# A sliding-window attention cut into 32 overlapped units, with half of its output product beside them

## What is computed

```python
def sliding_window_gqa_sinks(q, k, v, sinks):
    ...
    scores = jnp.einsum("bnqkgd,bnskd->bnkgqs", qb, kb) * scale
    scores = jnp.where(mask, scores, -jnp.inf)
    m = jnp.maximum(jnp.max(scores, axis=-1, keepdims=True), sink)
    p = jnp.exp(scores - m)
    denom = jnp.sum(p, axis=-1, keepdims=True) + jnp.exp(sink - m)
    out = jnp.einsum("bnkgqs,bnskd->bnqkgd", p / denom, vb)
...
h = h + (attn * jax.nn.silu(z)) @ w_out + b_out
h = rms_norm(h, final_norm_g)
hn = rmsnorm(h, norm_w[i])
proj = hn @ w_in[i]
```

## Time and profile before

| | us |
|---|---|
| median of 3 runs (3640.29 to 3643.76) | 3641.27 |
| the profiled execution | 3642.55 |
| its span, first to last instruction | 3640.7 |
| PE busy, of the span | 3226.1 |
| DVE busy | 1650.6 |
| ACT busy | 1090.1 |
| POOL busy | 830.5 |

### The profile page before, as it was taken

How to read it: one execution, slowest core, us unless ns; L and a number is a source line. 1 busy time by engine, 2 the same in 40 slices (tenths; PEclk the granted TensorE clock), 3 DMA queues, 4 the chain that set the end, 5 groups by cost and what they waited for, 6 DMA issues and landing times.

```text
span 3640.7 us, 37492 instructions
## 1 busy us (share of the span) xinstructions
PE 3226.1 (89%) x15228; PEld 2508.5 (69%) x15228; DVE 1650.6 (45%) x2650; ACT 1090.1 (30%) x1814; POOL 830.5 (23%) x655
## 2 busy tenths in 40 slices
PE   8999899999998999999996659789876898889978
PEld 6766676668777777788874437677754777667746
DVE  6977621124455443413344553476753344331233
ACT  2135531123411211233224431444431222221134
POOL 3210011114155642253110001111100223221211
PEclk9999899999999999999997789899988999789989
DMA  3110011114122321233110001210103233321111
GB/s 118 41 35 18 7 35 47 41 63 158 59 74 81 92 80 47 85 115 131 41 35 18 6 30 64 83 29 24 47 28 88 65 101 84 130 92 37 37 52 58
DMA packets 240171, 225.40 MB, mean 62 GB/s; under 512 B 14720, under 2 KB 197376, under 8 KB 238976
## 3 DMA queue, kind: packets, MB, share of 16 engines
q1 hardware_dynamic: 220720, 180.84, 16.4%
q10 hardware_dynamic: 19280, 42.18, 3.2%
HBM read 184.25 MB, written 38.73 MB: 61 GB/s over the span
## 4 chain that ended last, share of the span: by engine, by line
PE 67%; DVE 12%; ACT 7%; POOL 6%; issue 5%; DMA 2%; ACTq 0%; SPq 0%; DVEq 0%; POOLq 0%
PE psum L499 17%; PE psum L501 16%; PE psum L500 16%; PE psum L505 4%; PE psum L614 3%; POOL arena L2876 3%; POOL WS L2802 2%; DVE arena L2185 1%; DVE arena L2451 1%; DVE arena L2471 1%; PE psum L660 1%; PE psum L871 1%; PE psum L686 1%; ACT arena L1559 1%; PE psum L1066 1%
## 5 line engine op out<-in xcount | busy, mean ns | idle before, releaser
L2802 POOL TENSOR_TENSOR WS<-arena,WS 128x1024 fp32r<-128x1024 f32 x239 | 590.8, 2476 | 2305.5 <-ACT WS L1083 2305.4
L499 PE MATMUL psum<-XH,WS 128*128 128x512 f32 x2464 | 991.3, 402 | 36.8 <-POOL XL L2858 15.9
L500 PE MATMUL psum<-XL,WS 128*128 128x512 f32 x2464 | 967.7, 393 | 0.0
L501 PE MATMUL psum<-XH,WS 128*128 128x512 f32 x2464 | 967.7, 393 | 0.0
L499 PEld LDWEIGHTS psum<-XH,WS 128*128 128x128 f32 x2464 | 469.1, 190 | 154.6 <-issue 42.1
L501 PEld LDWEIGHTS psum<-XH,WS 128*128 128x128 f32 x2464 | 467.6, 190 | 100.2
L500 PEld LDWEIGHTS psum<-XL,WS 128*128 128x128 f32 x2464 | 469.1, 190 | 97.6 <-issue 4.3
L1083 ACT ACTIVATE WS<-arena 128x1024 fp32r<-128x1024 f32 x239 | 251.0, 1056 | 846.5 <-PE psum L501 333.0
L499 PE MATMUL psum<-WS,XH 128*128 128x512 f32 (+1 forms) x1024 | 402.5, 393 | 49.8 <-POOL WS L2802 35.5
L500 PE MATMUL psum<-WS,XH 128*128 128x512 f32 (+1 forms) x1024 | 397.1, 388 | 0.0
L501 PE MATMUL psum<-WS,XL 128*128 128x512 f32 (+1 forms) x1024 | 397.1, 388 | 0.0
(11 more groups left out here) (293 smaller groups left out, 3256.8 us busy)
## 6 DMA issues: line engine op xcount, KB each, us to landing
arena<-in_w_in SPq DMA_DIRECT2D x85, 512.0 KB, 3.8
arena<-in_w_in_even SPq DMA_DIRECT2D x48, 512.0 KB, 4.1
arena<-in_w_out SPq DMA_DIRECT2D x32, 512.0 KB, 3.3
arena<-in_w_out_even SPq DMA_DIRECT2D x32, 512.0 KB, 3.3
h_spill<-arena ACTq DMA_DIRECT2D x24, 512.0 KB, 3.4
arena<-h_spill ACTq DMA_DIRECT2D x12, 1024.0 KB, 9.2
arena<-s_table SPq DMA_DIRECT2D x8, 1536.0 KB, 6.8
arena<-in_w_in_odd SPq DMA_DIRECT2D x18, 512.0 KB, 3.8
```

Of the source, the lines that this page charges most:

```text
L499: e.matmul(ps, wh, xh, start=start, stop=False)
L500: e.matmul(ps, wh, xl, start=False, stop=False)
L501: return e.matmul(ps, wl, xh, start=False, stop=stop)
L2802: e.tensor_tensor(lo, raw(book.raw_of.get(("w", u), 0), kbs, n), hi.bitcast(F32), SUB).then_inc(*w.up("w_lo", u))
```

## The change

**The units.** The 16 steps of eight heads become 32 units of four heads, numbered by block of tokens first: four units (g, and which half of its heads) for block 0, four for block 1, and so on. They overlap by position in a common loop `attention2` of 37 rounds, called ticks here. In tick u, PE makes the scores of unit u, the transposes of u - 2 and the values of u - 3; DVE does the maximum of u, the division of u - 1 and the gating of u - 4; ACT copies the transposed probabilities of u - 2 (now both blocks of keys) and takes the exponentials of u. The buffers for probabilities are three, those for transposed ones two. PSUM banks are given as before: 0 to 3 to scores (two per unit), 4 and 5 to transposes (two per unit), 6 to the values, 7 to the products beside them.

**The work beside.** The four late z blocks do their first half before the loop and their second half in ticks 1, 3, 5 and 7. The output product of the first four token tiles runs inside the loop, one tile of 24 matmuls in each of the ticks 17, 19, 21, 23 (first 512 outputs) and 27, 30, 33, 34 (second). The engines that follow PE do their part one tick later. The product of the last four tiles follows the loop with `proj_th`.

**Splits, loads and norms.** ACT and POOL split `Z2` by blocks of tokens, in every fourth tick from 8 to 36; h comes back from DRAM by halves (ticks 16 and 32) into the space of the queries. The norms go by halves of the tokens too: `od_post(0)` beside the product of the last four tiles, `od_post(1)` after it and after the transposes of half 0.

```diff
+        UNITS = [(n, g, hq) for n in range(8) for g in range(2) for hq in range(2)]
+        PRU, PTU = [view(84 + 4 * i, 4, 256) for i in range(3)], [view(96 + 4 * i, 2, 512) for i in range(2)]
+        STU = [view(104 + i / 16, 12) for i in range(3)]
+        BO2, G2 = view(72, 2, 512), view(76, 2, 512)
+        SQ2 = [view(80, 2, 512), view(100, 2, 512)]
+        XS3 = view(84, 4, S)
+        FILL = (1, 3, 5, 7, 17, 19, 21, 23, 27, 30, 33, 34)
+        def H2(tile):
+            return QT[:, 2 * (tile % 4):2 * (tile % 4) + 2, half_of(tile // 4)]
+        def blocks_of(u):
+            return ([1], 128) if UNITS[u][0] == 0 else ([0, 1], 0)
+        def attention2(tick, fill, late):
+            for u in range(37):
+                tick(u)
+                if u - late in FILL:
+                    next(fill, None)
+            run(fill)
...
+            late = [load_w(w2[:, 1792 + 128 * i:1920 + 128 * i], 8, 128) for i in range(4)]
+            def z_tile(i, half, ring):
+                u, hl = late[i]
+                bank = take(ring, ("z2o_ps", 4 + i, half), ("z2o", 4 + i, half))
+                w.wait_ge("w_lo", u)
+                sl = half_of(half)
+                for kb in range(8):
+                    t = mm3(psum[:, bank, :], hl[0][:, kb, :], hl[1][:, kb, :], XH[:, kb, sl], XL[:, kb, sl], kb == 0, kb == 7)
+                t.then_inc(*w.up("z2o_ps", 4 + i, half, also=[("w_used", u)] if half else []))
+            for i in range(4):
+                z_tile(i, 0, pb)
...
+            def values2(u):
+                n, g, hq = UNITS[u]
+                kbs = blocks_of(u)[0]
+                bank = take(ob2, ("o2", u), ("zo2", u))
+                for kb in kbs:
+                    w.wait_ge("t2_out", u, kb)
                 w.wait_ge("v2", 7)
-                for p in range(2):
-                    for kb in kbs:
-                        t = e.matmul(psum[64 * p:64 * p + 64, bank, :], V2[:, n - 1 + kb, 64 * g:64 * g + 64],
-                                     pt_of(g, n)[:, 2 * p + kb, :], start=kb == kbs[0], stop=kb == 1)
-                t.then_inc(*w.up("o2", g, n))
-
-            def attend(g):
-                for n in range(8):
-                    if n and g == 0:
-                        output2(g, n - 1)
-                    scores2(g, n)
-                    if n and g == 1:
-                        output2(g, n - 1)
-                    yield
-                output2(g, 7)
-                yield
-            weave((attend(0), 1, True),
-                  (proj_cm("z2o_ps", (), w2, 1792, 4, b7, lambda m, half: [("z2o", m, half)], base=4), 1, True))
-            w.mark("od_a0")
-            run(attend(1))
-            w.mark("od_a1")
-            for event in (("od_a0", "act"), ("od_a0", "dve"), ("zo2", 1, 7)):
-                w.wait_ge(*event)
-            run(proj_tm("o3_ps", (0,), ap["w_out_odd_2"], 0, 512, pb, lambda tile: [("o3a", tile)], x="odo"))
-            run(proj_tm("o3_ps", (1,), ap["w_out_odd_2"], 512, 512, pb, lambda tile: [("o3b", tile)]))
-            w.mark("od")
-
-
-            turn_x("b3", view(52, 4, S))
+                for kb in kbs:
+                    for p in range(2):
+                        t = e.matmul(psum[64 * p:64 * p + 64, bank, 0:256], V2[:, n - 1 + kb, 64 * g:64 * g + 64],
+                                     PTU[u % 2][:, kb, 256 * p:256 * p + 256], start=kb == kbs[0], stop=kb == 1)
+                t.then_inc(*w.up("o2", u))
...
+            def tick(u):
+                if u < 32:
+                    scores2(u)
+                if 2 <= u < 34:
+                    turned2(u - 2)
+                if 3 <= u < 35:
+                    values2(u - 3)
+            def z_late():
+                for i in range(4):
+                    z_tile(i, 1, b7)
+                    ws.free()
+                    yield
+            w3 = ap["w_out_odd_2"]
+            attention2(tick, chain(z_late(), *[
+                proj_tm("o3_ps", (ch,), w3, 512 * ch, 512, b7, lambda tile, ch=ch: [("o3", ch, tile)], tiles=range(4),
+                        ready=lambda tile: ("odo", tile)) for ch in range(2)]), 0)
+            for ch in range(2):
+                run(proj_th("o3_ps", (ch,), w3, 512 * ch, 1, lambda tile: [("o3", ch, tile)], x="odo"))
...
+            def turned2(u):
+                for kb in blocks_of(u)[0]:
+                    w.wait_ge("t2", u, kb)
+                    if u >= 2:
+                        w.wait_ge("o2", u - 2)
+                    e.activation(PTU[u % 2][:, kb, :], ps_of("t2", u, kb), ACT.Copy).then_inc(
+                        *w.up("t2_ca", u, kb, also=[("t2_out", u, kb)]))
...
+            def tick(u):
+                if 2 <= u < 34:
+                    turned2(u - 2)
+                if u < 32:
+                    powers(u)
+                if u >= 8 and u % 4 == 0:
+                    n = u // 4 - 2
+                    w.wait_ge("zo2", u - 5)
+                    w.wait_ge("z2o_ps", 7, n // 4)
+                    e.activation(XH[:, :, tile_of(n)], Z2[:, :, tile_of(n)], ACT.Copy).then_inc(*w.up("x_hi", "odo", n))
+                if u == 16:
+                    load_h2(0, 15)
+                if u == 32:
+                    load_h2(1, 31)
+                    e.dma_start(BO2, row_in("b_out").rearrange("p (a b) -> p a b", a=2)).then_inc(*w.landed("od_rows", 0))
+                    e.dma_start(G2, row_in("final2").rearrange("p (a b) -> p a b", a=2)).then_inc(*w.landed("od_rows"))
+            def fill():
+                for i in range(4):
+                    z_ev(4 + i, 1)
+                    ws.free()
+                    if i == 3:
+                        for _ in range(4):
+                            ws.load()
+                    yield
+                for ch in range(2):
+                    for tile in range(4):
+                        if tile == 3:
+                            for _ in range(4):
+                                ws.free()
+                            if ch == 0:
+                                for _ in range(4):
+                                    ws.load()
+                        yield
+            attention2(tick, fill(), 1)
...
+            weave((chain(proj_th(), proj_th()), 1, True), (od_post(0), 1, True))
+            turn_half("b3", 0, lambda kb: col("norm_w_3", kb), [])
+            run(od_post(1))
+            turn_half("b3", 1, lambda kb: col("norm_w_3", kb), [])
...
+            def gated2(u):
+                n, g, hq = UNITS[u]
+                z = Z2[:, 4 * g + 2 * hq:4 * g + 2 * hq + 2, tile_of(n)]
+                w.wait_ge("o2", u)
+                for k in range(2):
+                    w.wait_ge("z2o", 4 * g + 2 * hq + k, n // 4)
+                e.tensor_tensor(z, z, psum[:, book.bank("o2", u), 0:256].rearrange("p (a b) -> p a b", a=2), M).then_inc(
+                    *w.up("zo2", u))
+            def tick(u):
+                if u < 32:
+                    weigh(u)
+                if 1 <= u < 33:
+                    divide(u - 1)
+                if 4 <= u < 36:
+                    gated2(u - 4)
...
+            def od_post(hf):
+                for j in range(7):
+                    tile = 4 * hf + j
+                    if j < 4:
+                        h = H2(tile)
+                        w.wait_ge("od_rows")
+                        w.wait_ge("o3", 1, tile)
+                        e.tensor_tensor(h, h, BO2, A_).then_inc(*w.up("o3_b", tile))
+                    if 1 <= j < 5:
+                        h, r = H2(tile - 1), small[:, 31 + tile:32 + tile]
+                        nrm_recip("odf", tile - 1, r)
+                        w.own()
+                        e.scalar_tensor_tensor(h, h, r, G2, M, M).then_inc(*w.up("h2", tile - 1))
+                    if j < 4:
+                        nrm_mean("odf", tile, small[:, 32 + tile:33 + tile], 1e-5)
+                    if 2 <= j < 6:
+                        nrm_mean("b3", tile - 2, small[:, 2 * tile - 4:2 * tile - 3], 1e-6)
+                    if j >= 3:
+                        r = small[:, 2 * tile - 6:2 * tile - 5]
+                        nrm_recip("b3", tile - 3, r)
+                        w.own()
+                        if hf:
+                            w.wait_ge("turn", "b3", 7, 0)
+                        e.tensor_scalar(XS3[:, j - 3, :].rearrange("p (a b) -> p a b", a=2), H2(tile - 3), r, None, M).then_inc(
+                            *w.up("nrm_xs", "b3", tile - 3))
+                    yield
+            run(od_post(0))
+            for ch in range(2):
+                for tile in range(4, 8):
+                    o3(ch, tile)
+            turn_half("b3", 0, lambda kb: col("norm_w_3", kb))
+            run(od_post(1))
+            turn_half("b3", 1, lambda kb: col("norm_w_3", kb))
...
+            def tick(u):
+                if u >= 8 and u % 4 == 0:
+                    n = u // 4 - 2
+                    w.wait_ge("x_hi", "odo", n)
```

(2 more changed lines are left out.)

390 lines of the change are left out of this document (168 added, 222 removed).

## The result

The changed kernel takes 3657.44 us (median of 6 runs, 3653.93 to 3660.11), the kernel before 3642.49 (6 runs, 3640.25 to 3648.63). The ratio is 1.0039, with a 95% interval of 1.0026 to 1.0052: slower by 0.26% to 0.52%. I had forecast 3608, with a range of 3585 to 3634.

A forecast was written before the change was run, and what follows sets the result against it. PE bounds most of the kernel, but a chain of dependences sets the second attention's time. Terms 272.1 + 5.5 + 2 + 9 + 50.2 + 31.8 = 370.6 us against 403.6, -33, gave 3608 us, range 3585 to 3634.

The forecast's parts named there:

- step 1: Attention loop: each tick is a full round of scores, DVE's whole tick and values, 6.24 us per unit of four heads.
- The rival that this round isn't there: Attention loop: values not held by the gating, about 4.05 us a tick, about 3545 us in all; chance 0.04.
- step 5: Attention loop: part of the ticks run at the lower clock, 1.9 us more each; +9 us (0 to 59).
- The rival of the half clock: Attention loop: clock stays at half, all 31 ticks cost 1.9 us more, 59 instead of 9, 3658 us; chance 0.05.
- steps 3 and 4: Attention loop: ACT's four weight splits at tick 24 delay the next division, +5.5 us; one VectorE division held behind POOL, +2.
- step 6: Output product's last four tiles, after the loop: PE waits 4.5 us for block 7's split; 50.2 us in all.
- step 7: From the output product's end to the third layer's first product: 31.8 us against 30.0, halving the norms gains nothing.
- That nothing outside the stretch changes: Rest of the kernel: no edit touches anything outside the stretch, so only the stretch's time was forecast to change, by -33 us.
- the stretch: From the second attention's first scores to the third layer's first product: 370.6 us forecast against 403.6 before.

## Why the prediction was wrong, point by point

**The round of waits (step 1)** was right: 6.23 us against 6.24, with PE's values released by the gating in every tick from 4 to 31. That it fits to the hundredth is luck, as the values took 1.08 where I had 0.94 and small errors in the other terms gave it back. The gating took 0.41 (estimated 0.42). The rival that this round isn't there fell. What I didn't do was to ask what it would take to remove it; one line did.

**The clock (step 5)** is the step that failed, in its size. I had +9 us for the whole loop. In ticks 9 to 31, the fifteen ordinary ticks were 6.89 on average, 0.65 over 6.24, in sum 9.7; and the six with a tile were 14.85 against 11.68, in sum 19.0. That is 28.7 in these ticks. The kernel with six extra matmuls takes nearly all of it back: ticks 9 to 30 are 209.0 us in the changed kernel and 183.3 there. What stays is mostly in ticks 10 and 26, which follow the two stalls and are 7.2 and 7.8 us there too, so some 2.5 of the 28.7 are not the clock's. Ticks 0 to 8 are 12 us over the forecast, and 7 of these are three z tiles that start at the half clock (8.4, 7.5 and 7.5 us in ticks 3, 5 and 7, against 5.44).

Two errors are in it. I started from 30% of the ticks, and then halved that because tiles would keep the clock up. They do so for the ticks between them (6.9 us on average, 7.5 in the kernel without tiles), but each tile starts at the half clock and pays more than that for it. And I priced the lower clock only in scores and values, not in the tiles, which are the longest pieces on the path. The share at the half clock stayed at what the earlier trace rows said, 42%.

**The rival of the half clock** had the right mechanism and 0.05 of the chances. I gave it a threshold (22 of 31 ticks) computed from scores and values alone, and set its chance as if it were all or nothing, while a clock at 0.79 all the way was the plain continuation of the row. That its 3658 us lies next to the measured 3657.4 is luck. It has 1.9 us more in each of 31 ticks, and they had 0.65 without a tile and 3.2 with one, and 10 us came from the third layer.

**ACT and POOL (steps 3 and 4)** cost 10.4 us together in ticks 9 and 25 (22.9 against 12.5), where I had 7.5, but it was POOL both times. DVE's small operations stood behind POOL's, 4.1 us in tick 9 and 3.6 in tick 25; ACT's stall lay beneath: its four weight splits took 11.3 us, but the next division didn't wait for the exponentials, as I had said it would. The Trainium skill (SBUF — State Buffer, "Who interferes with whom") says that a VectorE instruction with two SBUF inputs contends with a GpSimd instruction that reads SBUF. The operation L2504 with its two inputs of four columns, held for 2.12 us, agrees.

I had also misread the trace of before when I wrote that no row shows more than one hit. In the half of the attention with z tiles, each of POOL's four weight splits held the divisions. Eight of them take 2.19 us undisturbed and 4.28 beside three of the splits (3.75 beside the first, with half the keys). One such case, DVE and then POOL:

```profile
1950.23 4.28 DVE L2471 TENSOR_SCALAR arena<-arena 128x256 f32<-128x256 f32 x8
```

```profile
1950.78 2.52 POOL L2802 TENSOR_TENSOR WS<-arena,WS 128x1024 fp32r<-128x1024 f32 x1 [35.47 <-ACT WS L1083]
```

**The last four tiles (step 6)** were right: 51.0 against 50.2, the wait 5.28 against 4.5, on POOL's split as said. **The tail (step 7)** was 32.4 against 31.8, though 1.3 of it was the wait for a bank, which I hadn't seen, so the rest of the estimate was a little high.

**That nothing outside the stretch changes** was wrong by 10 us. The program there is the same; its time is not. Of the 48 us between forecast and profile, the stretch has 39 and the third layer 10, less 1 us by which the changed kernel reached the stretch earlier.

## What to carry to other kernels

When units are overlapped by position, follow one resource of one unit (here the bank of the values) around all engines. If its release stands at the end of an engine's turn and its next use ahead of the next unit's start, the turns run one after the other, whatever the overlap looks like. Put the releases first in each turn. Price work that follows a pause at the clock that the pause leaves, and the longest such pieces first. Before a stall is given to one engine, look whether a second one lies beneath it.

## What the runs showed of the hardware

- Useless matmuls in PE's pauses made a kernel 29 us faster, with the granted clock of the loop at 0.94 instead of 0.79.
- Eight matmuls of 64 rows and 256 columns that all use the lower 64 rows took 3.72 us, 0.46 each; the scores, which alternate between the two halves of the rows and between two banks, take 0.28 each (1.13 for four). No run parts these two differences.
- A DVE operation on four columns took up to 2.27 us while POOL worked on 1024.
- The third layer of the kernel before, with the same instructions, took 1333.5 us in three profiles, within 0.2 (one of them with matmuls added that end 26 us ahead), and 1338.0 in one profile after six small matmuls that end 14 us ahead.
